# A four-layer decoder trunk on one core: where the residual shifts of the last layer stand on ScalarE, and where the forget decay stands on VectorE

## The chip, the cores and the metric

The kernel runs on one core of a Trainium2 chip. The metric is the device time of one execution in microseconds (us). TensorE (PE in the profile) does the matrix products, VectorE (DVE) and ScalarE (ACT) the work between them, GpSimd (POOL) a small part, and SyncE (SP) issues the transfers. Each engine runs its own list of instructions in order and waits on semaphores for the others.

## What is computed

272 tokens (16 meta tokens and 256 of the sequence) of width 1024 go through four layers. Each layer is a mixer and a gated feed-forward part, each with a residual and a layer norm. The mixers are of the kinds fox, swa, mla, fox: layer 0 and layer 3 are forgetting attention, the part that matters here.

```
def fox_mixer(h, w_in, b_f, w_o):
    proj = h @ w_in
    q, k, v, fg = jnp.split(proj, [hd, 2 * hd, 3 * hd], axis=-1)
    log_f = jax.nn.log_sigmoid((fg + b_f).astype(jnp.float32))
    c = jnp.cumsum(log_f, axis=1)
    o = dense_causal_attention(q, k, v, c)      # logits + c[t] - c[s]
    return o.reshape(B, L, hd) @ w_o
...
h = layer_norm(DEEPNORM_ALPHA * h + mix, ln1_g[i], ln1_b[i])
ffn = conv_glu_ffn(h, ...)
h = layer_norm(DEEPNORM_ALPHA * h + ffn, ln2_g[i], ln2_b[i])
```

The 16 forget gates of a token need `h @ w_in[:, 3072:]` in full precision, then a log-sigmoid and a running sum over the tokens. That sum is the decay.

## The kernel before

**Products and weights.** Tokens lie along the free dimension (272 columns), channels along the 128 partitions. Weights come from memory in units of 128 x 1024, through a ring of four buffers (`raw`, `w_hi`, `w_lo`). ScalarE rounds a unit to `w_hi` (L796, `split_hi`), VectorE subtracts to get `w_lo` (L1166 in `split_lo`), and TensorE makes each product of three passes, hi x hi, hi x lo and lo x hi (L376, L379, L380, `panel`; L415 to L429 in the leading panels that follow a layer norm chunk by chunk). One panel is 8 chunks x 3 passes = 24 matmuls into a PSUM bank. The splits run three units ahead of the panel (`AHEAD`). A split of a unit waits until TensorE has begun the panel that shows the ring buffer to be free (`w_used`). A new transfer waits for the `w_lo` of four units before.

**The fox stage.** Stage "v" makes 8 value panels (banks 0 to 3), stage "qk" 16 panels, queries and keys in turn (banks 0 and 1). VectorE copies each value panel out of its bank with `take_v` (L1356, "q_rope<-ps" in the rows, since the buffer is shared), which counts up `bank_free`. TensorE then turns the value to token order (L480, `value`), three panels late: value 0 after panel 3, value 4 after panel 7, and values 5, 6 and 7 within the first two panels of "qk". The first panel of "qk" waits for seven copies (`bank_free`, copy 6 among them, counted from 0).

**The gates.** After panel 2, TensorE computes the gate logits in full float32 (L608, 8 products that show as 16 rows). In layer 3 these read the residual `h` after its shift, so TensorE waits there for all eight `affine` instructions (L911), in which ScalarE adds the layer norm's beta to `h` for one chunk each. The panels themselves read `h_hi` and `h_lo`, which contain beta already. In layer 0 there is no such wait. Behind panel 3, ScalarE does five small instructions on 16 partitions (L933 to L937), and then VectorE does the rest of the log-sigmoid, the running sum (L1345) and two rounded copies of it in `dec` (L1348 and the subtraction behind it). The first scores of the stage (L502) read `dec`, after the first two panels of "qk".

**What sets the order.** The program of each engine is written out by hand. In the fox value stage, the loop of VectorE's `gemm` does for every panel j: the `split_lo` of a unit, then `before(i, j)`, then the wait for the panel, then the evicting copy. ScalarE's loop does for every panel m: `split_hi`, then three, three and two `affine` for m = 0, 1, 2 (layer 3 only), then the copies of turned values.

Of the kernel before, what the change touches and what calls it, by code (L numbers as in the profile page):

```python
# [31 lines left out]
DC = D // P  # L32
# [151 lines left out]
def build_program(nc, x, weights, consts, out):  # L184
    with ExitStack() as ctx:
        def sb(name, shape, dt=F32):
            return ctx.enter_context(nc.sbuf_tensor(name, shape, dt))
# [6 lines left out]
        h, squares = h_all[:, 0:DC], h_all[:, DC:DC + 2]  # L194
# [25 lines left out]
        y = sb("y", [P, 4, T])  # L220
        gated = sb("gated", [P, T])
# [73 lines left out]
        def bank(p, n=BANKS):  # L295
            return ps[:, p % n, 0:T]
# [17 lines left out]
        def turns(eng, n, emit, first=0):  # L314

            if n - first == 1:
                emit(first)
            elif n > first:
                with eng.Fori(first, n) as i:
                    emit(i)  # L320
# [466 lines left out]
        def _(act):  # L787
# [40 lines left out]
            def copy_value(m, where):  # L828
                act.wait_ge(v_turned, n_v[0] + m + 1)
                b = ps[:, where]  # L830
                act.activation(v_tok[0:16, 2, m * P:(m + 1) * P], b[0:16, 2 * P:3 * P], ACT.Copy)
                act.activation(v_tok[:, 0:2, m * P:(m + 1) * P],
                               b[:, 0:2 * P].rearrange("p (c n) -> p c n", c=2), ACT.Copy).then_inc(v_copied, 1)
# [33 lines left out]
            def split_panel(a, name, j):  # L867
                for u in units_of(a, name, 0, j):
                    split_hi(u)
# [37 lines left out]
            def affine(n, ks):  # L907

                for k in ks:
                    act.wait_ge(h_ready, 8 * (n + 1) + k + 1)  # L910
                    act.activation(h[:, k, :], h[:, k, :], ACT.Identity,  # L911
                                   bias=ln_par[:, n, 1, k:k + 1]).then_inc(affine_done, 1)
# [9 lines left out]
            for a, kind in enumerate(KINDS):  # L922
                if kind == "fox":
                    pq = LAYERS[a]["qk"][2]

                    def gate_act_ops():

                        z, mag, e, u1, lnu = (y[0:16, 0, :], y[0:16, 1, :], y[0:16, 2, :], y[0:16, 3, :],
                                              gated[0:16, :])
                        act.wait_ge(gate_done, n_fox + 1)  # L930
                        gb = CONST["gate_b"][0] + n_fox
                        bias = cst[0:16, gb:gb + 1]
                        act.activation(z, ps[0:16, 6, 0:T], ACT.Identity, bias=bias)  # L933
                        own.link(act.activation(mag, ps[0:16, 6, 0:T], ACT.Abs, bias=bias))
                        own.link(act.activation(e, mag, ACT.Exp, scale=-1.0))
                        own.link(act.activation(u1, e, ACT.Identity, bias=1.0))
                        act.activation(lnu, u1, ACT.Ln).then_inc(gate_act, 1)  # L937

                    for m in range(PAIRS):
                        split_panel(a, "v", m)  # L940
                        if a and m < 3:
                            affine(2 * a - 1, range(3 * m, min(DC, 3 * m + 3)))
                        if m == 1 and a == 0:
                            act.wait_ge(const_landed, 16)
                            act.wait_ge(init_done, INITS)
                        if m >= 3:
                            copy_value(m - 3, 4 + (m - 3) % 2)
                        if m == 3:
                            gate_act_ops()
# [211 lines left out]
        def _(dve):  # L1161
# [3 lines left out]
            def tt(out_, a_, b_, op):  # L1165
                return dve.tensor_tensor(out_, a_, b_, op)  # L1166

            def split_lo(u, slot):
                dve.wait_ge(hi_ready, u + 1)
                tt(w_lo[slot][:], raw[slot][:], w_hi[slot][:].bitcast(F32), ALU.subtract).then_inc(lo_ready, 1)  # L1170

            def split_units(layer, name, i, j):
                s, u0, _ = LAYERS[layer][name]
                for u in s.new_units(j):
                    first = u0 + u + AHEAD
                    if isinstance(i, int) and i * s.body_units + first >= N_UNITS:
                        continue
                    split_lo(i * s.body_units + first, first % RING)

            def gemm(layer, name, evac, links=0, before=None, straight=False, late=None):  # L1180

                s, u0, p0 = LAYERS[layer][name]

                def turn(i):
                    if links is not None:
                        own.turn(i, links)
                    for j in range(s.body):
                        ending = late is not None and i == s.turns - 1 and j == s.body - 1
                        last_unit = (s.units - 1 + u0 + AHEAD, (s.units - 1 + u0 + AHEAD) % RING)
                        if not ending:  # L1190
                            split_units(layer, name, i, j)
                        else:
                            for u in s.new_units(j)[:-1]:
                                if i * s.body_units + u0 + u + AHEAD < N_UNITS:
                                    split_lo(i * s.body_units + u0 + u + AHEAD, (u0 + u + AHEAD) % RING)
                            late()
                        if before is not None:
                            before(i, j)
                        dve.wait_ge(panel_done, i * s.body + (p0 + j + 1))
                        evac(i, j, bank(p0 + j + s.shift), i * s.body + (p0 + j))  # L1200
                        if ending and last_unit[0] < N_UNITS:
                            split_lo(*last_unit)

                if straight:
                    for i in range(s.turns):
                        turn(i)
                else:
                    turns(dve, s.turns, turn)
                if links is not None:
                    own.turned(s.turns)  # L1210
# [110 lines left out]
            for a, kind in enumerate(KINDS):  # L1321
                if kind == "fox":
                    pq = LAYERS[a]["qk"][2]

                    def decay():

                        z, mag, e, u1, lnu = (y[0:16, 0, :], y[0:16, 1, :], y[0:16, 2, :], y[0:16, 3, :],
                                              gated[0:16, :])
                        zero = squares[0:16, 0, :]
                        dve.wait_ge(gate_act, n_fox + 1)  # L1330
                        own.link(dve.tensor_scalar(u1, u1, -1.0, None, ALU.add))
                        own.link(dve.tensor_scalar(zero, u1, 0.0, None, ALU.is_equal))
                        tt(lnu, lnu, zero, ALU.add)
                        own.link(tt(u1, u1, zero, ALU.add))
                        own.link(dve.reciprocal(u1, u1))
                        own.link(tt(lnu, lnu, u1, ALU.mult))
                        own.link(tt(lnu, lnu, e, ALU.mult))
                        own.link(dve.tensor_scalar(z, z, -1.0, 0.0, ALU.mult, ALU.max))
                        own.link(tt(lnu, lnu, z, ALU.add))
                        own.link(dve.tensor_scalar(zero, zero, 0.0, 1.0, ALU.mult, ALU.add))  # L1340
                        if a == 0:
                            own.link(copy(pick[:], c("pick")))
                        row = scores[0:16, 0, :]
                        total = row[:, SCOL[2]:SCOL[3]]
                        own.link(dve.tensor_tensor_scan(total, zero, lnu, 0.0, ALU.mult, ALU.add))  # L1345
                        copy(row[:, SCOL[0]:SCOL[1]], total[:, 0:CHUNKS[0][1]])
                        own.link(copy(row[:, SCOL[1]:SCOL[2]], total[:, 0:CHUNKS[1][1]]))
                        own.link(copy(dec[0:16], row))  # L1348
                        tt(dec[32:48], row, dec[0:16].bitcast(F32), ALU.subtract).then_inc(decay_done, 1)
# [7 lines left out]

                    def before_v(i, j):

                        if i * 4 + j == 4:  # L1360
                            if a == 0:
                                dve.wait_ge(const_landed, 16)
                                dve.wait_ge(init_done, INITS)
                                own.link(dve.tensor_scalar(neg_sinks[:], c("sinks"), -1.0, None, ALU.mult))
                            decay()

                    gemm(a, "v", take_v, links=None, before=before_v, straight=True)
                    n_v += 8

                    def take_k(m):  # L1370
# [326 lines left out]
```

## Time and profile before

| | |
|---|---|
| median of 3 runs | 1399.6 us (1399.28 to 1401.74) |
| the profiled execution | 1400.15 us |
| its span, first to last instruction | 1398.3 us |
| mean granted TensorE clock | 0.984 of full speed |
| TensorE busy | 1333.4 us, 95% |
| VectorE, ScalarE, GpSimd busy | 945.4, 811.4, 231.7 us |

The profiled execution has 1.85 us outside its span. A busy TensorE is not one at its peak: matmuls are pipelined, and a row's duration overlaps the next row's. The pace is read from one start to the next. Starts are in us from the span's beginning.

### The profile page before, as it was taken

How to read it: one execution, taken by the hardware profiler on the slowest of the kernel's cores; microseconds unless marked ns; L12 is line 12 of the kernel's file. 1: busy time of each engine (PE TensorE's matmuls, PEld its weight loads, DVE VectorE, ACT ScalarE, POOL GpSimd, SP SyncE). 2: the span in 40 equal slices, each digit the busy share in tenths (PEclk: the TensorE clock that was granted, in tenths of full speed). 3: DMA queues.
4: the chain of work that ended last, by engine and by line, in shares of the span. 5: the costliest groups of instructions: out<-in, count | busy, mean ns of one | idle time of the engine just before them, and what ended most of it. 6: DMA issues, size and time to landing. Idle time of an engine off the chain costs nothing.

```text
span 1398.3 us, 30127 instructions
## 1 busy us (share of the span) xinstructions
PE 1333.4 (95%) x10433; PEld 1264.9 (90%) x10433; DVE 945.4 (68%) x1890; ACT 811.4 (58%) x1637; POOL 231.7 (17%) x216
## 2 busy tenths in 40 slices
PE   7899999999999999999977999999998999999997
PEld 6788999999977999999965899999997888999997
DVE  4665777765797777765684777776565566777754
ACT  5455676654666666654743567665454555766544
POOL 1000044420000044320010003433000000243400
PEclk9999999999999999999996999999999999999999
DMA  7332456556421456556431235655643333356662
GB/s 261 111 108 74 135 178 184 180 181 195 137 76 48 135 181 191 170 191 187 127 97 31 61 121 166 184 176 183 194 130 125 107 93 122 121 188 187 183 215 84
DMA packets 56867, 203.33 MB, mean 145 GB/s; under 512 B 6224, under 2 KB 8272, under 8 KB 56656
## 3 DMA queue, kind: packets, MB, share of 16 engines
q1 hardware_dynamic: 56784, 202.21, 46.2%
q8 instruction: 54, 0.88, 0.3%
q14 instruction: 29, 0.24, 0.0%
HBM read 201.13 MB, written 1.05 MB: 145 GB/s over the span
## 4 chain that ended last, share of the span: by engine, by line
PE 84%; DVE 7%; ACT 6%; issue 2%; DMA 1%; SPq 0%; DVEq 0%; ACTq 0%
PE ps L376 23%; PE ps L380 22%; PE ps L379 22%; PE ps L525 3%; PE ps L543 2%; DVE w_lo L1166 2%; PE ps L508 1%; PE ps L490 1%; ACT w_hi L796 1%; PE ps L415 1%; PE ps L421 1%; PE ps L418 1%; ACT probs L846 1%; DMA cst<-in_consts 1%; ACT L898 1%
## 5 line engine op out<-in xcount | busy, mean ns | idle before, releaser
L1166 DVE TENSOR_TENSOR w_lo<-raw,w_hi 128x1024 fp32r<-128x1024 f32 x378 | 462.5, 1225 | 251.6 <-ACT w_hi L796 250.0
L376 PE MATMUL ps<-h_hi,w_hi 128*128 128x272 f32 (+1 forms) x1752 | 511.2, 292 | 7.5 <-DVE q_rope L1356 4.9
L796 ACT ACTIVATE w_hi<-raw 128x1024 fp32r<-128x1024 f32 x378 | 396.8, 1051 | 188.9 <-PE ps L376 177.7
L380 PE MATMUL ps<-h_hi,w_lo 128*128 128x272 f32 (+1 forms) x1752 | 504.6, 288 | 0.0
L379 PE MATMUL ps<-h_lo,w_hi 128*128 128x272 f32 (+1 forms) x1752 | 503.2, 287 | 0.0
L376 PEld LDWEIGHTS ps<-h_hi,w_hi 128*128 128x128 f32 x1752 | 330.4, 189 | 15.5 <-issue 5.9
L379 PEld LDWEIGHTS ps<-h_lo,w_hi 128*128 128x128 f32 x1752 | 331.0, 189 | 0.3
L380 PEld LDWEIGHTS ps<-h_hi,w_lo 128*128 128x128 f32 x1752 | 330.5, 189 | 0.0
L376 PE MATMUL ps<-hid_hi,w_hi 128*128 128x272 f32 (+2 forms) x676 | 197.0, 291 | 2.7 <-DVE keys L1166 1.3
L380 PE MATMUL ps<-hid_hi,w_lo 128*128 128x272 f32 (+2 forms) x676 | 194.6, 288 | 0.0
L379 PE MATMUL ps<-hid_lo,w_hi 128*128 128x272 f32 (+2 forms) x676 | 194.6, 288 | 0.0
L1140 POOL TENSOR_TENSOR gated<-y 128x272 f32<-128x272 f32 x88 | 134.8, 1532 | 276.4 <-DVE y L1555 261.8
L1117 POOL TENSOR_TENSOR h<-h,y 128x272 f32<-128x272 f32 x24 | 17.9, 773 | 779.6 <-ACT y L895 779.6
L1090 ACT ACTIVATE y<-ps,cst 128x272 f32<-128x272 f32 x176 | 100.1, 569 | 65.6 <-PE ps L380 60.9
L376 PEld LDWEIGHTS ps<-hid_hi,w_hi 128*128 128x128 f32 x676 | 128.4, 190 | 4.8 <-DVE keys L1166 2.0
L379 PEld LDWEIGHTS ps<-hid_lo,w_hi 128*128 128x128 f32 x676 | 128.8, 191 | 0.1
L380 PEld LDWEIGHTS ps<-hid_hi,w_lo 128*128 128x128 f32 x676 | 128.7, 190 | 0.0
L846 ACT ACTIVATE probs<-scores,stats 16x16 f32<-16x16 f32 (+2 forms) x192 | 76.9, 401 | 58.9 <-DVE stats L1226 58.9
L1553 DVE SCALAR_TENSOR_TENSOR y<-ps,cst,y 128x271 f32<-128x271 f32 x176 | 87.4, 496 | 31.6 <-ACT y L1090 25.3
L1555 DVE SCALAR_TENSOR_TENSOR y<-ps,cst,y 128x270 f32<-128x270 f32 x176 | 87.8, 499 | 26.8 <-DVE y L1553 25.1
L380 PE MATMUL ps<-hid,w_lo 128*128 128x272 f32 (+1 forms) x288 | 82.2, 285 | 0.0
L379 PE MATMUL ps<-hid,w_hi 128*128 128x272 f32 (+1 forms) x288 | 82.1, 285 | 0.0
(159 smaller groups left out, 1722.9 us busy)
## 6 DMA issues: line engine op xcount, KB each, us to landing
raw<-in_weights SPq DMA_DIRECT2D x378, 512.0 KB, 3.6
cst<-in_consts SPq DMA_DIRECT2D x1, 1795.5 KB, 11.7
h<-in_x SPq DMA_DIRECT2D x2, 544.0 KB, 5.4
out<-h SPq DMA_DIRECT2D x8, 128.0 KB, 1.8
```

The lines of the kernel that those rows point to most:

```text
L376: m = pe.matmul(b, whi, xhi, start=n == 0, stop=False)
L379: pe.matmul(b, whi, xlo, start=False, stop=False)
L380: m = pe.matmul(b, wlo, xhi, start=False, stop=n == len(tiles) - 1)
L525: return pe.transpose(b[0:keys_n, col:col + q], pr[0:q, c0:c0 + keys_n], ident[0:q, 0:q])
L543: ins = pe.matmul(ps[HD * s:HD * s + HD, 6, lo:T], v_tok[:, t, col:col + HD], probs_t[:, s, c0:c0 + T - lo], start=n == 0, stop=n == 2)
L796: act.activation(w_hi[slot][:], raw[slot][:], ACT.Copy).then_inc(hi_ready, 1)
L846: ins = act.activation(probs[0:r, hn % 4, PCOL[ch]:PCOL[ch] + hi], scores[0:r, s, SCOL[ch]:SCOL[ch + 1]], ACT.Exp, scale=-1.0, bias=stats[ ...
L1090: act.activation(y[:, j, :], bank(pu + j), ACT.Identity, scale=col(2), bias=col(3)).then_inc(conv_begun, 1)
L1140: pool.tensor_tensor(gated[:], y[:, 2 * slot, :], y[:, 2 * slot + 1, :], ALU.mult).then_inc(gate_mul, 1)
L1166: return dve.tensor_tensor(out_, a_, b_, op)
L1553: own.link(dve.scalar_tensor_tensor(yj[:, 1:T], b[:, 0:T - 1], col(1), yj[:, 1:T], ALU.mult, ALU.add))
L1555: dve.scalar_tensor_tensor(yj[:, 2:T], b[:, 0:T - 2], col(0), yj[:, 2:T], ALU.mult, ALU.add).then_inc(bank_free, 1)
```

## The change

Two edits, both of order. The number of instructions on every engine is the same, and TensorE's order is the same.

1. ScalarE, layer 3: all eight `affine` stand behind the first `split_hi` of the value stage. Before, they were spread in groups behind its first, second and third.
2. VectorE, layers 0 and 3: `decay`, one block ahead of the eviction of panel 4, becomes four pieces. `decay_guard` stays there, `decay_quotient` (the reciprocal) stands ahead of the eviction of panel 5, `decay_steps` ahead of that of panel 6, and `decay_rows` (running sum and `dec`) behind the eviction of panel 7, ahead of the "qk" loop.

```
@@ -938,8 +938,8 @@
                     for m in range(PAIRS):
                         split_panel(a, "v", m)
-                        if a and m < 3:
-                            affine(2 * a - 1, range(3 * m, min(DC, 3 * m + 3)))
+                        if a and m == 0:
+                            affine(2 * a - 1, range(DC))
@@ -1322,22 +1322,32 @@
-                    def decay():
+                    def decay_guard():
+
                         dve.wait_ge(gate_act, n_fox + 1)
                         own.link(dve.tensor_scalar(u1, u1, -1.0, None, ALU.add))
                         own.link(dve.tensor_scalar(zero, u1, 0.0, None, ALU.is_equal))
                         tt(lnu, lnu, zero, ALU.add)
                         own.link(tt(u1, u1, zero, ALU.add))
+
+                    def decay_quotient():
+
                         own.link(dve.reciprocal(u1, u1))
+
+                    def decay_steps():
+
                         own.link(tt(lnu, lnu, u1, ALU.mult))
                         own.link(tt(lnu, lnu, e, ALU.mult))
                         own.link(dve.tensor_scalar(z, z, -1.0, 0.0, ALU.mult, ALU.max))
                         own.link(tt(lnu, lnu, z, ALU.add))
                         own.link(dve.tensor_scalar(zero, zero, 0.0, 1.0, ALU.mult, ALU.add))
+
+                    def decay_rows():
+
                         if a == 0:
                             own.link(copy(pick[:], c("pick")))
                         row = scores[0:16, 0, :]
@@ -1357,14 +1367,20 @@
                     def before_v(i, j):
-                        if i * 4 + j == 4:
+                        m = i * 4 + j
+                        if m == 4:
...
-                            decay()
+                            decay_guard()
+                        if m == 5:
+                            decay_quotient()
+                        if m == 6:
+                            decay_steps()
                     gemm(a, "v", take_v, links=None, before=before_v, straight=True)
+                    decay_rows()
                     n_v += 8
```

On ScalarE, this is the start of layer 3's value stage, behind the roundings of `h` (`h_hi`), as a difference from before to changed. `w_hi` rows are weight splits, `h<-h,cst` rows the residual shifts.

```order
 L906 ACTIVATE h_hi<-h,cst 128x272 x8
 L796 ACTIVATE w_hi<-raw 128x1024
-L911 ACTIVATE h<-h,cst 128x272 x3
-L796 ACTIVATE w_hi<-raw 128x1024
-L911 ACTIVATE h<-h,cst 128x272 x3
-L796 ACTIVATE w_hi<-raw 128x1024
-L911 ACTIVATE h<-h,cst 128x272 x2
-L796 ACTIVATE w_hi<-raw 128x1024
+L911 ACTIVATE h<-h,cst 128x272 x8
+L796 ACTIVATE w_hi<-raw 128x1024 x3
```

The shifts of chunks 3 to 7 now stand ahead of two weight splits that they stood behind.

On VectorE in layer 0, before: from the reciprocal to the eviction of panel 4 (the last row). Layer 3 has the same rows without the `pick` row.

```order
L1335 RECIPROCAL y<-y 16x272
L1166 TENSOR_TENSOR gated<-gated,y 16x272 x2
L1338 TENSOR_SCALAR y<-y 16x272
L1166 TENSOR_TENSOR gated<-gated,y 16x272
L1340 TENSOR_SCALAR h<-h 16x272
L1342 CAST pick<-cst 128x16
L1345 SCALAR_TENSOR_TENSOR scores<-h,gated 16x272
L1346 COPY scores<-scores 16x16
L1347 COPY scores<-scores 16x144
L1348 CAST dec<-scores 16x432
L1166 TENSOR_TENSOR dec<-scores,dec 16x432
L1356 COPY q_rope<-ps 128x272
```

The same place in the changed kernel, from the end of `decay_guard` to the weight split behind the eviction of panel 6. The copies "q_rope<-ps" are, in turn, the evictions of panels 4, 5 and 6.

```order
L1166 TENSOR_TENSOR y<-y,h 16x272
L1366 COPY q_rope<-ps 128x272
L1166 TENSOR_TENSOR w_lo<-raw,w_hi 128x1024
L1339 RECIPROCAL y<-y 16x272
L1366 COPY q_rope<-ps 128x272
L1166 TENSOR_TENSOR w_lo<-raw,w_hi 128x1024
L1166 TENSOR_TENSOR gated<-gated,y 16x272 x2
L1345 TENSOR_SCALAR y<-y 16x272
L1166 TENSOR_TENSOR gated<-gated,y 16x272
L1347 TENSOR_SCALAR h<-h 16x272
L1366 COPY q_rope<-ps 128x272
L1166 TENSOR_TENSOR w_lo<-raw,w_hi 128x1024
```

And right behind that, from the eviction of panel 7 to the first key copy of the "qk" stage.

```order
L1366 COPY q_rope<-ps 128x272
L1352 CAST pick<-cst 128x16
L1355 SCALAR_TENSOR_TENSOR scores<-h,gated 16x272
L1356 COPY scores<-scores 16x16
L1357 COPY scores<-scores 16x144
L1358 CAST dec<-scores 16x432
L1166 TENSOR_TENSOR dec<-scores,dec 16x432
L1166 TENSOR_TENSOR w_lo<-raw,w_hi 128x1024 x2
L1390 COPY keys<-ps 128x272
```

The running sum and the two `dec` rows moved from ahead of the eviction of panel 4 to behind that of panel 7. The reciprocal and the five steps after it now stand behind one and two evictions.

## Rows read from the trace of the kernel before

**Rows 1.** The page, busy us (share of the span) and instructions.

```profile
PE 1333.4 (95%) x10433; PEld 1264.9 (90%) x10433; DVE 945.4 (68%) x1890; ACT 811.4 (58%) x1637; POOL 231.7 (17%) x216
```

**Rows 2.** Waits, PE: who waited for whom, us in total, times, longest.

```profile
PE ps L376 <- DVE q_rope L1356: 4.9, 2, 2.5
...
PE ps L608 <- ACT h L911: 3.6, 1, 3.6
...
PE ps L480 <- DVE q_rope L1356: 2.5, 2, 1.4
```

**Rows 3.** Timeline, PE, layer 0: start, us, line, operation, count, idle and releaser.

```profile
18.80 3.84 PE L608 MATMUL ps<-h,cst 128*16 128x272 f32 x16
22.57 0.39 PE L376 MATMUL ps<-h_hi,w_hi 128*128 128x272 f32 x1
...
38.96 0.29 PE L380 MATMUL ps<-h_hi,w_lo 128*128 128x272 f32 x1
40.69 0.49 PE L480 MATMUL ps<-cst,q_rope 128*16 128x128 f32 x3 [1.44 <-DVE q_rope L1356]
...
43.65 0.39 PE L376 MATMUL ps<-h_hi,w_hi 128*128 128x272 f32 x1 [2.47 <-DVE q_rope L1356]
...
52.82 0.63 PE L502 MATMUL ps<-dec,pick 128*128 128x432 f32 x2 [0.37 <-DVE keys L1374]
```

**Rows 4.** Timeline, DVE, layer 0, around the decay block.

```profile
32.48 0.29 DVE L1331 TENSOR_SCALAR y<-y 16x272 f32<-16x272 f32 x1
...
33.95 1.84 DVE L1335 RECIPROCAL y<-y 16x272 f32<-16x272 f32 x1
35.83 0.89 DVE L1166 TENSOR_TENSOR gated<-gated,y 16x272 f32<-16x272 f32 x2
...
37.86 0.17 DVE L1342 CAST pick<-cst 128x16 fp32r<-128x16 f32 x1
...
40.19 0.44 DVE L1356 COPY q_rope<-ps 128x272 f32<-128x272 f32 x1
...
43.16 0.44 DVE L1356 COPY q_rope<-ps 128x272 f32<-128x272 f32 x1
```

**Rows 5.** Timeline, DVE, layer 3: running sum and the eviction of panel 4.

```profile
1071.69 0.71 DVE L1345 TENSOR_TENSOR_SCAN scores<-h,gated 16x272 f32<-16x272 f32 x1
...
1073.81 0.44 DVE L1356 COPY q_rope<-ps 128x272 f32<-128x272 f32 x1
```

**Rows 6.** Timeline, PE, layer 3, at the gates and at the first qk panel.

```profile
1047.45 0.29 PE L429 MATMUL ps<-h_hi,w_lo 128*128 128x272 f32 x1
1051.32 2.00 PE L608 MATMUL ps<-h,cst 128*16 128x272 f32 x4 [3.59 <-ACT h L911]
...
1056.60 0.39 PE L376 MATMUL ps<-h_hi,w_hi 128*128 128x272 f32 x1
...
1077.27 0.39 PE L376 MATMUL ps<-h_hi,w_hi 128*128 128x272 f32 x1 [2.47 <-DVE q_rope L1356]
```

**Rows 7.** Timeline, ACT, layer 3: shifts and weight splits.

```profile
1044.86 1.33 ACT L911 ACTIVATE h<-h,cst 128x272 f32<-128x272 f32 x3
1047.20 1.06 ACT L796 ACTIVATE w_hi<-raw 128x1024 fp32r<-128x1024 f32 x1 [1.01 <-PE ps L425]
...
1050.35 0.92 ACT L911 ACTIVATE h<-h,cst 128x272 f32<-128x272 f32 x2
```

**Rows 8.** Windows: stretch, its us, then busy us of PE, PEld, DVE, ACT, POOL, granted clock, DMA share, GB/s.

```profile
44.00:48.00 4.00, 4.00 (x22) 4.00 (x21) 2.30 (x3) 1.06 (x1) 0.00 (x0) 0.57 0.88 294
1051.00:1054.00 3.00, 2.68 (x6) 0.88 (x7) 1.05 (x2) 0.27 (x1) 0.00 (x0) 0.50 0.69 232
1078.00:1082.00 4.00, 4.00 (x22) 3.98 (x21) 1.92 (x3) 0.82 (x1) 0.00 (x0) 0.57 0.84 286
709.70:716.00 6.30, 3.95 (x24) 3.07 (x23) 6.06 (x13) 0.82 (x1) 2.38 (x3) 1.00 0.00 0
```

**Rows 9.** Timeline, PE, latent attention of layer 2, inside the last of those windows.

```profile
713.86 0.70 PE L704 MATMUL ps<-y,cst 128*128 128x272 f32 x2 [2.22 <-DVE queries L1166]
```

More of the change, by code:

```diff
@@ L1323, in _ @@
                     pq = LAYERS[a]["qk"][2]
-                    def decay():
-                        z, mag, e, u1, lnu = (y[0:16, 0, :], y[0:16, 1, :], y[0:16, 2, :], y[0:16, 3, :],
-                                              gated[0:16, :])
-                        zero = squares[0:16, 0, :]
+                    z, mag, e, u1, lnu = (y[0:16, 0, :], y[0:16, 1, :], y[0:16, 2, :], y[0:16, 3, :],
+                                          gated[0:16, :])
+                    zero = squares[0:16, 0, :]
+                    def decay_guard():
                         dve.wait_ge(gate_act, n_fox + 1)
```

## The prediction

> **What bounds the kernel now.** I read the page first: TensorE is busy 95% of the span [rows 1], so a microsecond counts only where TensorE stands still or runs slowly. The list of TensorE's waits comes second. Three of its lines lie in the code that the change touches [rows 2]: the first "qk" panel waits twice for a value eviction, 2.5 us each time; the turn of value 4 waits for one (two waits, 1.4 us the longer); and the gate logits of layer 3 wait 3.6 us for the residual shifts. Third, the timelines of TensorE, VectorE and ScalarE around these waits show what is late. In layer 0 TensorE's last value panel ends at 38.96 + 0.29 = 39.25. It idles 1.44 us, turns value 4, idles 2.47 us, and starts the first "qk" panel at 43.65 [rows 3]. VectorE meanwhile goes through the decay block from 32.48 to 40.19, 7.7 us on 16 partitions, and only then starts the evictions [rows 4]. Panels 4, 5 and 6 had been finished long before. Layer 3 shows the same 2.47 us [rows 6].
>
> The fourth view is the windows, for the granted clock. It is at its upper level (2.4 GHz) in most of the program, and falls to the lower one (1.2 GHz) right after each of the three stalls: 0.57 as a mean over 44 to 48 and over 1078 to 1082, and 0.50 over 1051 to 1054 [rows 8]. So each stall is paid twice, as idle time and as slow matmuls behind it. The price of the second part can be read from the gates, which are the same work in both layers: they take 22.57 - 18.80 = 3.77 us in layer 0 at the full clock [rows 3] and 1056.60 - 1051.32 = 5.28 us in layer 3 at the lower one [rows 6], 1.51 us more. For the "qk" panels, a mean clock of 0.57 over 4.00 us is at most 4.00 x 0.43 = 1.7 us lost. I take 1.5 us for each of the three places.
>
> **Edit 1, the shifts in layer 3.** Three shifts take 1.33 us and the last row has its full 0.5 us, so one follows another every (1.33 - 0.50) / 2 = 0.415 us [rows 7]. Eight in a row from 1044.86 end at 1044.86 + 7 x 0.415 + 0.5 = 1048.27. Before, the last ended at 1050.35 + 0.92 = 1051.27 and TensorE started at 1051.32. The gates start 3.0 us earlier. TensorE's leading panels end at 1047.45 + 0.29 = 1047.74 [rows 6], so 0.6 us of idle stays out of 3.59, and the clock should not fall there: another 1.5 us. The cost is on ScalarE: the second weight split, which started at 1047.20 after 1.01 us of idle for TensorE, now starts at 1048.2, and the third stands directly behind it, ahead of no shift any more. The `w_lo` of the second moves by 1 us on VectorE, and so do the evictions of panels 1 and 2 queued behind them and the transfers that SP's queue issues on them. TensorE covers this with 3.77 us of gates and a value panel of about 3 us before it wants the second of those units, so I cost it at nothing. Without this cover it would be the 1 us. Edit 1 is worth 3.0 + 1.5 = 4.5 us.
>
> **Edit 2, the decay pieces.** The first "qk" panel waits for the eviction of panel 6, so I count what stands ahead of that copy on VectorE. The guard ends at 33.95. The reciprocal takes 35.83 - 33.95 = 1.88, the steps 37.86 - 35.83 = 2.03, the rows 40.19 - 37.86 = 2.33 (with the `pick` copy), and a pair of eviction and weight split (43.16 - 40.19) / 2 = 1.49 [rows 4]. Before: 33.95 + 1.88 + 2.03 + 2.33 + 2 x 1.49 = 43.17. After: the same sum without the rows, 33.95 + 1.49 + 1.88 + 1.49 + 2.03 = 40.84. TensorE follows 0.49 later (43.16 to 43.65), at 41.3. The gain in layer 0 is 2.33 us. In layer 3 the rows have no `pick` and take 1073.81 - 1071.69 = 2.12 us [rows 5]. That is the gain there.
>
> Where the stall goes: value 4 no longer waits, since the eviction of panel 4 starts at 33.95. Its turn follows the last value panel at once and ends near 39.6. What is late next is still the eviction of panel 6, so TensorE idles about 41.3 - 39.6 = 1.7 us once, against 1.44 + 2.47 = 3.91 us in two parts. Whether the clock still falls has to be bounded from both sides. It fell after 1.44 and 2.47 us of idle with only turns between them [rows 3, 8]. It stayed at 1.00 from 709.7 to 716.0 with an idle of 2.22 us inside [rows 8, 9]. The 1.7 us that stays is below that, so I take no fall: 1.5 us more in each layer. The other end is nothing.
>
> The Trainium skill ("TensorE: Matmul & The Clock Gate", section "Why this matters for your kernels") advises against idle gaps over about 3 us. The trace departs from it: no single gap at the "qk" panel was over 2.47 us, and the clock fell. By the page alone edit 2 could bring no clock back, since there was no long gap, and the sum would be 3 us smaller.
>
> The rows piece is the one with a new place: behind it on VectorE are now two weight splits and the first key copy, and TensorE's first scores wait for `dec`. In layer 0 the eviction of panel 6 starts at 40.84, that of panel 7 at 42.33. Its copy takes some 0.36, and the rows end at 42.69 + 2.33 = 45.0. The scores started at 52.82 [rows 3]; moved forward by 2.3 + 1.5 us they start at 49.0. So `dec` has 4.0 us of slack, the two splits and a key copy (about 2.8 us) fit behind it, and the cost is nothing. Without that cover each microsecond late is one in each layer.
>
> **The sum.** Edit 1 brings 3.0 + 1.5. Edit 2 brings 2.33 + 1.5 in layer 0 and 2.12 + 1.5 in layer 3. Together this is 11.95 us. From the profiled execution's 1400.15 us that gives 1388.2 us. That execution is 0.55 us above the median, so by the median it would be 1387.65. I put the time at 1388.0.
>
> **Rivals.**
> - *The clock still falls at the "qk" panel.* Between the last value panel's matmuls and the first of "qk" there remain a turn of 0.49 us and 1.7 us of idle, 2.2 us without an ordinary matmul, about as much as the 2.22 us that did no harm at 713.86. If the moment decides, one or both places lose their 1.5 us: 1389.5 or 1391.0. The Trainium skill (same page, "Part 4: PE-mode transpose") says that transposes do not count as busy in the usual way; that speaks for this rival. Chance 0.27.
> - *Gains given back downstream.* The latent stage of layer 2 has stretches at the lower clock too, and everything behind layer 0 starts 3.8 us earlier. Runs of before spread over 1399.28 to 1401.74, so such things move the time by 1 to 2.5 us: up to 1390.5, or down to 1385.5. Chance 0.10, either side.
> - *The idle belongs to something else.* If the gate's wait ended with something other than the shifts, or the "qk" panel's with its weights, edit 1 or 2 would bring nothing: 1388.0 + 4.5 = 1392.5 without edit 1 and 1388.0 + 7.45 = 1395.5 without edit 2. Against it: ScalarE ends the last shift at 1051.27, 0.05 us before TensorE starts, and the weights of the first "qk" panel were split a whole pair before its eviction. Chance 0.05.
> - *Slower: `dec` comes too late.* The rows piece stands behind all evictions, so if it ran so much longer there that it ended after 49.0, the scores of both layers would wait. It decides from 4.0 us of delay per layer. To end above 1399.6 it would have to eat 11.95 us on top, thus be (11.95 + 2 x 4.0) / 2 = 10 us late in each layer, five times its own length. At 12 us late each it would give 1388.2 + 2 x 8 = 1404. Chance 0.01.
>
> **How the numbers follow.** My forecast, 1388.0 with a range of its own of 1386.5 to 1389.5, gets 0.57. With the clock rival the time reaches 1391. Adding the spread on the low side and the far end of the downstream rival gives 1385.5 to 1391.8, with somewhat over 1 in 10 outside. A difference under 0.2%, 2.8 us, cannot be told from none. All cases but the last, and a combination of lost edits inside the fourth, are beyond that: faster 0.96, same 0.03, slower 0.01.
>
> **What would show it.** In the changed profile the wait of the gates for the shifts is under 1 us, the gates take 3.8 us, and the clock is at 1.00 behind them. Value 4 has no wait. The first "qk" panel of both layers waits once, 1.7 us, for a value eviction; the copy of panel 6 starts 2.3 us (layer 0) earlier. `dec` is ready at about 45 and the first scores of layer 0 start at 49.0. The prediction is wrong if the clock falls in these places, if the first scores wait for `dec`, or if TensorE waits for a weight split in layer 3's first four panels.

## The result: 1.0% faster, a little more than forecast, and the profile after

The changed kernel takes 1385.83 us in the median of four runs (1384.12 to 1387.86), the one before 1400.38 us (1399.28 to 1401.74, with a fourth run that was taken beside it): a ratio of 0.9896, 95% interval 0.9879 to 0.9914. The forecast was 1388.0, with 1386.5 to 1389.5 as the range of its own mechanism and 1385.5 to 1391.8 with the rivals added: the time lies outside the first and 0.3 us inside the second. The profiled execution took 1384.12 us, with a span of 1382.2 us, 16.1 us less than the one of before.

The page of the changed kernel: TensorE has 9.5 us less of busy time for the same 10433 instructions, so the single instruction took less on average.

```profile
PE 1323.9 (96%) x10433; PEld 1258.4 (91%) x10433; DVE 945.0 (68%) x1890; ACT 810.9 (59%) x1637; POOL 231.7 (17%) x216
```

TensorE's waits in the changed kernel (us in total, times, longest) answer to [rows 2]. The wait for the first "qk" panel is 1.8 and 1.5 us instead of 2.5 twice, that for the shifts 0.6 instead of 3.6, and the wait of value 4 is gone.

```profile
PE ps L376 <- DVE q_rope L1366: 3.3, 2, 1.8
...
PE ps L608 <- ACT h L911: 0.6, 1, 0.6
```

Its timeline of TensorE (start, duration, then the idle time ahead), layer 0 first and then layer 3 (from 1031.05 on), answers to [rows 3] and [rows 6].

```profile
39.14 0.49 PE L480 MATMUL ps<-cst,q_rope 128*16 128x128 f32 x3
41.38 0.40 PE L376 MATMUL ps<-h_hi,w_hi 128*128 128x272 f32 x1 [1.75 <-DVE q_rope L1366]
...
50.55 0.63 PE L502 MATMUL ps<-dec,pick 128*128 128x432 f32 x2 [0.36 <-DVE keys L1390]
...
1031.05 0.39 PE L415 MATMUL ps<-h_hi,w_hi 128*128 128x272 f32 x1 [0.57 <-ACT h_hi L906]
...
1040.93 3.84 PE L608 MATMUL ps<-h,cst 128*16 128x272 f32 x16 [0.58 <-ACT h L911]
1044.70 0.39 PE L376 MATMUL ps<-h_hi,w_hi 128*128 128x272 f32 x1
...
1063.26 0.40 PE L376 MATMUL ps<-h_hi,w_hi 128*128 128x272 f32 x1 [1.54 <-DVE q_rope L1366]
...
1070.92 0.63 PE L502 MATMUL ps<-dec,pick 128*128 128x432 f32 x2 [0.37 <-DVE keys L1390]
```

Layer 0 has its first "qk" panel at 41.38 (forecast 41.3). Its first scores (L502) start at 50.55 instead of 52.82: 2.27 us, the decay's part alone. In layer 3 the gates take 3.77 us (1040.93 to 1044.70) against 5.28, and from their end to the first "qk" panel it is 18.56 us against 20.67.

The windows of the changed kernel (columns as in [rows 8]; the mean granted clock, as a share of the upper level, is the third number from the end) show why: the clock fell again in layer 0, and did not in layer 3, neither at the gates nor at the first "qk" panel.

```profile
42.00:46.00 4.00, 4.00 (x22) 3.97 (x21) 3.83 (x9) 0.93 (x1) 0.00 (x0) 0.57 0.45 136
1041.00:1045.00 4.00, 4.00 (x18) 1.70 (x19) 3.06 (x4) 1.77 (x2) 0.00 (x0) 1.00 0.37 107
1060.00:1067.00 7.00, 5.46 (x45) 5.15 (x44) 6.70 (x15) 2.00 (x5) 0.00 (x0) 1.00 0.50 153
```

VectorE in layer 0 of the changed kernel, evictions of panels 4 to 7 (L1366), reciprocal (L1339), the start of the steps (the 0.89 row) and the weight split behind the rows piece, stands as it was counted from [rows 4], within 0.05 us.

```profile
34.00 0.44 DVE L1366 COPY q_rope<-ps 128x272 f32<-128x272 f32 x1
...
35.49 1.83 DVE L1339 RECIPROCAL y<-y 16x272 f32<-16x272 f32 x1
37.36 0.44 DVE L1366 COPY q_rope<-ps 128x272 f32<-128x272 f32 x1
...
38.85 0.89 DVE L1166 TENSOR_TENSOR gated<-gated,y 16x272 f32<-16x272 f32 x2
...
40.88 0.44 DVE L1366 COPY q_rope<-ps 128x272 f32<-128x272 f32 x1
...
42.37 0.43 DVE L1366 COPY q_rope<-ps 128x272 f32<-128x272 f32 x1
...
45.04 1.23 DVE L1166 TENSOR_TENSOR w_lo<-raw,w_hi 128x1024 fp32r<-128x1024 f32 x1
```

ScalarE runs the eight shifts in one piece of 3.40 us, as counted from [rows 7].

```profile
1037.48 3.40 ACT L911 ACTIVATE h<-h,cst 128x272 f32<-128x272 f32 x8
1040.79 1.99 ACT L796 ACTIVATE w_hi<-raw 128x1024 fp32r<-128x1024 f32 x2
```

**Where the 16.1 us went.** The span can be cut into stretches from one marker on TensorE to the next: from the start to the first scores of layer 0; from there to the first leading panel of layer 3 (L415 at 1038.42 before), called the middle stretch from here on; from there to the first scores of layer 3 (layer 3's stretch); and the rest. Two of the markers in the kernel before:

```profile
1038.42 0.39 PE L415 MATMUL ps<-h_hi,w_hi 128*128 128x272 f32 x1 [0.57 <-ACT h_hi L906]
...
1086.44 0.63 PE L502 MATMUL ps<-dec,pick 128*128 128x432 f32 x2 [0.36 <-DVE keys L1374]
```

| stretch | before | changed | difference |
|---|---|---|---|
| to the first scores of layer 0 | 52.82 | 50.55 | -2.27 |
| middle stretch, from there to layer 3's leading panels | 985.60 | 980.50 | -5.10 |
| from there to the first scores of layer 3 | 48.02 | 39.87 | -8.15 |
| from there to the end of the span | 311.86 | 311.28 | -0.58 |

Layer 3 gave 8.15 us against a forecast of 4.5 + 2.12 + 1.5 = 8.12. Layer 0 gave 2.27 of 3.83. The 5.10 us in between were not forecast, and no instruction differs there. 4.00 of them lie between two turns of the latent attention of layer 2, which each follow a wait of 5.7 us. The two rows of before, and then the two of the changed kernel:

```profile
738.12 0.80 PE L480 MATMUL ps<-cst,q_rope 128*16 128x128 f32 x3 [5.67 <-issue]
...
757.78 0.80 PE L480 MATMUL ps<-cst,q_rope 128*16 128x128 f32 x3 [5.68 <-issue]
```

```profile
735.58 0.80 PE L480 MATMUL ps<-cst,q_rope 128*16 128x128 f32 x3 [5.69 <-issue]
...
751.24 0.80 PE L480 MATMUL ps<-cst,q_rope 128*16 128x128 f32 x3 [5.69 <-issue]
```

From one turn to the other it is 19.66 us at a mean granted clock of 0.59 before, and 15.66 us at 0.83 in the changed kernel.

### The profile page after: what moved, and what is told of

It is laid out like the page before. It is cut to its first block, busy times and chain, and to the rows that moved or that the text cites. A ratio compares the mean times of both kernels' runs of the same rounds, so it can differ in the third digit from the quotient of the medians.

```text
span 1382.2 us, 30127 instructions
## 1 busy us (share of the span) xinstructions
PE 1323.9 (96%) x10433; PEld 1258.4 (91%) x10433; DVE 945.0 (68%) x1890; ACT 810.9 (59%) x1637; POOL 231.7 (17%) x216
## 4 chain that ended last, share of the span: by engine, by line
PE 80%; DVE 8%; ACT 6%; issue 3%; POOL 1%; DMA 1%; ACTq 0%; SPq 0%; DVEq 0%; POOLq 0%
PE ps L376 22%; PE ps L380 21%; PE ps L379 21%; PE ps L525 3%; PE ps L543 2%; DVE w_lo L1166 2%; PE ps L508 1%; ACT w_hi L796 1%; ACT probs L846 1%; PE ps L490 1%; PE ps L415 1%; POOL gated L1140 1%; PE ps L421 1%; PE ps L418 1%; DMA cst<-in_consts 1%
```

## The experiments

Medians are given with the range of the runs. Each group of runs has runs of the kernel before beside it, and the ratio is to these.

### Edit 1 alone

```
 (before)
-if a and m < 3:
-    affine(2 * a - 1, range(3 * m, min(DC, 3 * m + 3)))
+if a and m == 0:
+    affine(2 * a - 1, range(DC))
```

> The kernel before with edit 1 alone (the eight shifts of layer 3 behind the first weight split). My theory: the gates start 3.0 us earlier and run at the full clock (3.8 us against 5.3), so 4.5 us less than before, near 1395.9 us against a median of before of 1400.4; the decay stalls stay, with their fall of the clock. Rival A (the affine wait is worth only its idle time, the clock falls anyway): 3.0 us less. Rival B (the surplus that the changed kernel showed in the latent stage of layer 2 belongs to its position or its order): since nothing differs up to layer 3, the latent stage must then look exactly like that of before, six windows at the lower clock; if the surplus is chance from one execution to the next, the windows at the lower clock differ although the program up to there is the same.

Measured: 1392.46 us (1392.13 to 1396.66), before 1399.96, ratio 0.9955 (0.9939 to 0.9972), which is 3.9 to 8.5 us less; this contains the 4.5, though the medians lie 7.5 us apart. In the trace the gates start 9.89 us behind the first leading panel instead of 12.90 and take 3.77 us instead of 5.28: 4.5 us. The decay stall of layer 3 is as it was, but the clock falls sooner and for longer than in the trace of before: over the 7 us from 1.75 us ahead of the first "qk" panel it has a mean of 0.52, where before has 0.76. This takes back 0.89 us (10.06 us from that panel to the first scores, against 9.17), so layer 3's stretch is 44.38 us, only 3.64 less than before.

```profile
1068.00:1075.00 7.00, 5.25 (x23) 5.25 (x24) 4.41 (x6) 1.06 (x1) 0.00 (x0) 0.52 0.75 239
```

For rival B: up to layer 3 this is the kernel before, and yet the middle stretch takes 982.50 us, not 985.60. It varies without any change, and its 3.10 us are part of what the medians show beyond 4.5.

### Edit 2 alone

```
 (changed)
-if a and m == 0:
-    affine(2 * a - 1, range(DC))
+if a and m < 3:
+    affine(2 * a - 1, range(3 * m, min(DC, 3 * m + 3)))
```

> The kernel before with edit 2 alone (decay in four pieces in layers 0 and 3). My theory: 2.3 us in layer 0 and 2.1 us in layer 3 for certain, and 1.5 us more in each layer in which the clock does not fall at the first qk panel: between 4.4 and 7.4 us less than before, middle 5.9, near 1394.5. In the gates of layer 3 the wait of 3.6 us and the slow 5.3 us stay. Rival (the gains of the two edits are not additive, because the shorter layer 0 changes where the clock falls later): the sum of this gain and that of edit 1 alone differs from 14.5 us by more than 3 us.

Measured: 1392.19 us (1388.75 to 1394.39), ratio 0.9940 (0.9923 to 0.9957), 6.0 to 10.8 us less. The expected 4.4 to 7.4 us overlap this, though the medians lie 7.8 us apart. The two ratios multiply to 0.9955 x 0.9940 = 0.9895, and the changed kernel has 0.9896: nothing speaks against the edits adding, within intervals that are each 4.6 to 4.8 us wide. The trace: first scores of layer 0 at 50.36, with a fall of the clock as in the changed kernel; layer 3's stretch 44.58 us, 3.44 less than before (2.1 and the clock); 986.19 us between.

### Decay in two pieces

```
 (changed)
 if m == 4:
     ...
     decay_guard()
-if m == 5:
     decay_quotient()
-if m == 6:
     decay_steps()
```

> The changed kernel, but with the decay in two pieces only: guard, quotient and steps all ahead of the eviction of panel 4 as before, the rows behind that of panel 7. My theory: what counts is only how much stands ahead of the eviction of panel 6, which is the same as with four pieces, so the first qk panel starts at the same 41.4 us and the time is that of the changed kernel within 0.5 us (near 1386). Rival (the interleaving itself matters, since values 4 and 5 come free earlier and the stall lies in one part): the eviction of panel 4 starts at 37.9 instead of 34.0, value 4 still does not wait (it is wanted at 39.1), so at most a few tenths; if it is over 1 us slower, interleaving has a worth of its own.

Measured: 1388.57 us (1383.44 to 1390.07), ratio 0.9913 (0.9892 to 0.9933). The median lies 2.7 us above the changed kernel's, which by itself would meet the rival's mark of 1 us, but the intervals overlap and the trace puts the difference elsewhere. Timeline of TensorE, layer 0: the first "qk" panel waits 1.76 us and starts at 41.47, against 1.75 and 41.38.

```profile
39.22 0.49 PE L480 MATMUL ps<-cst,q_rope 128*16 128x128 f32 x3
41.47 0.40 PE L376 MATMUL ps<-h_hi,w_hi 128*128 128x272 f32 x1 [1.76 <-DVE q_rope L1366]
...
49.13 0.63 PE L502 MATMUL ps<-dec,pick 128*128 128x432 f32 x2 [0.37 <-DVE keys L1388]
```

Value 4 is turned without a wait here too. Layer 3's stretch is 39.87 us, the same as in the changed kernel. So in the fox layers two pieces are as good as four: only what stands ahead of the eviction of panel 6 counts. The clock did not fall in layer 0 this time, and the scores start 1.42 us before the changed kernel's, although the same instructions stand ahead of the eviction of panel 6. The middle stretch was slow, 986.10 us. That this has nothing to do with the pieces is not shown by one trace.

### Steps behind the evictions too

```
 (changed)
-if m == 6:
-    decay_steps()
 ...
 gemm(a, "v", take_v, ...)
+decay_steps()
 decay_rows()
```

> The changed kernel with the five steps moved too, behind the eviction of panel 7 ahead of the rows. My theory: the eviction of panel 6 starts at 38.9 instead of 40.9 us, before TensorE wants it, so the stall of 1.75 us at the first qk panel is gone and with it every fall of the clock there. On VectorE the rows still end near 45.1, so the two weight splits and the first key copy end near 47.8, later than TensorE wants the first scores (46.6): a new wait of about 1.2 us in place of 0.4. Net about 1.2 us less per layer, and 1.5 us more in a layer in which the clock fell: 2.4 to 5.4 us less than the changed kernel, near 1382. Rival (the stall only moves): the first scores wait the full 1.75 us more and the time is that of the changed kernel, 1386.

Measured: 1386.52 us (1381.88 to 1388.12), ratio 0.9898 (0.9879 to 0.9917). The expected 2.4 to 5.4 us under the changed kernel did not come: against 1385.83 the medians show no gain. The trace shows the mechanism as expected: no wait at the first "qk" panel in either layer, no fall of the clock, and the first scores waiting 1.24 us for the key copy, at 48.10.

```profile
48.10 0.62 PE L502 MATMUL ps<-dec,pick 128*128 128x432 f32 x2 [1.24 <-DVE keys L1389]
```

This is 2.4 us ahead of the changed kernel in layer 0 (0.9 us ahead of its repetition below, in which the clock did not fall), and layer 3's stretch is 38.52 us against 39.87, 1.35 less. The middle stretch took 986.79, 6.3 us more than in the trace of the changed kernel, which is more than the fox layers gained.

### The changed kernel again

> The changed kernel once more, unaltered, as a control beside the next three. Theory 1 (the surplus over the forecast of 12 us was chance: the latent stage of layer 2 had 17 us at the lower clock in that execution, 27 in the one of before): the median comes out near 1387.5, 12 to 13 us under before, and from the first scores of layer 0 to the first leading panel of layer 3 it takes anything from 980 to 987 us. Theory 2 (the surplus belongs to the change): again 14.5 us or more under before, and that stretch stays near 980.5.

Measured: 1383.88 us (1383.22 to 1385.27), before 1399.5, ratio 0.9889 (0.9871 to 0.9907). The median, 15.6 us under before, speaks for theory 2. The trace speaks for a mixture: the middle stretch took 982.41 us, again on the short side of the 980 to 987, and the clock did not fall in layer 0 (first scores at 48.98, where 49.0 had been forecast, and 1.57 us before the first trace of the same kernel). Over the two groups and the two-piece kernel, with the same timing in the fox layers, the medians are 1383.9, 1385.8 and 1388.6, which is 15.6, 14.6 and 11.4 us under the runs of before beside them. I take it that the change is worth 11 to 16 us, and these runs do not narrow it. The times of the 35 runs of before beside the experiments go with their mean granted clock, 0.982 to 0.990 (correlation -0.73), which fits a spread that comes from the clock.

### The latent stage filled

```
 (changed)
+def keep_warm(count, where):
+    for _ in range(count):
+        pe.matmul(ps[:, where, T:512], h_hi[:, 0, 0:P], h_hi[:, 1, 0:512 - T], ...)
 ...
 latent_panel(0, 0)
+keep_warm(16, 4)
 swap(gated[:], pa + 6)
 ...
 if m == 0:
+    keep_warm(12, 4)
     swap_rope(1)
 ...
+if m in (ROPE_AFTER, ROPE_AFTER + 1):
+    pe.wait_ge(o_split, PAIRS * a + m - ROPE_AFTER)
+    keep_warm(36, 6)
```

> The changed kernel, with extra matmuls on TensorE (into unused columns, their results are not read) inside its four long waits in the latent stage of layer 2: 16, 12, 36 and 36 of 240 columns. No work is left out and the waits themselves stay. Theory 1 (the clock of that stage explains both the surplus and the spread of the runs): the granted clock stays at its upper level there, the stretch from the first scores of layer 0 to layer 3 falls under 980 us, to about 973, and the spread of the runs shrinks to 2 or 3 us; time near 1377. Theory 2 (the stage is held by VectorE and the clock there costs nothing): the clock stays up, the stretch does not change, the time is that of the changed kernel. Third possibility: the extra matmuls do not fit in the waits and push the stage back, slower by up to 5 us.

Measured: 1381.50 us (1379.22 to 1384.12), ratio 0.9876 (0.9856 to 0.9897). The median is 2.4 us under the changed kernel's beside it, with intervals that overlap. The added wait (`o_split`) keeps the filler out of a PSUM bank that VectorE still reads. The windows of the stage, 695 to 775 us, one line each, of the kernel before, the changed kernel and this one, show the mean granted clock in the third number from the end.

Kernel before:

```profile
695.00:775.00 80.00, 61.09 (x362) 48.84 (x361) 56.26 (x168) 33.33 (x97) 4.40 (x4) 0.83 0.25 73
```

Changed kernel:

```profile
695.00:775.00 80.00, 60.56 (x398) 48.49 (x396) 60.88 (x192) 35.22 (x109) 4.40 (x4) 0.89 0.24 73
```

Latent stage filled:

```profile
695.00:775.00 80.00, 70.70 (x530) 59.38 (x528) 63.73 (x202) 38.78 (x124) 4.40 (x4) 1.00 0.23 71
```

The clock stays at its upper level throughout, and the middle stretch takes 977.13 us. In every trace this stage is the only part of the middle stretch with a lower clock: cut into 50 us from the first scores of layer 0 on, all the other slices are at 1.00. In the table over all traces the stretch gets shorter as the clock rises, in the main though not row by row, while TensorE's instructions in it are the same in all but the filled ones:

| trace | clock, 695 to 775 | middle stretch, us |
|---|---|---|
| edit 2 alone | 0.81 | 986.19 |
| before | 0.83 | 985.60 |
| two pieces | 0.83 | 986.10 |
| steps behind | 0.83 | 986.79 |
| edit 1 alone | 0.87 | 982.50 |
| key copy first (below) | 0.87 | 981.10 |
| stalls filled (below) | 0.89 | 982.42 |
| changed, repeated | 0.89 | 982.41 |
| changed | 0.89 | 980.50 |
| shifts first (below), filled | 0.98 | 978.09 |
| both (below), filled | 1.00 | 977.73 |
| latent stage filled | 1.00 | 977.13 |

So theory 1 holds for the mechanism: the surplus of the changed kernel's trace over the forecast is granted clock in the latent stage. Its size was less than I gave it: 977, not 973. The ends of the waits stay where VectorE's rotary work puts them (its last row ahead of the first turn ends at 734.21, the turn starts at 734.31). What is left idle is 0.9 us at the swaps and 1.7 us at the turns, where it had been 2.2 to 2.7 and 5.7. TensorE's timeline of this run has the turns.

```profile
734.31 0.49 PE L480 MATMUL ps<-cst,q_rope 128*16 128x128 f32 x3 [1.67 <-issue]
748.49 0.49 PE L480 MATMUL ps<-cst,q_rope 128*16 128x128 f32 x3 [1.68 <-issue]
```

The spread of the runs did not shrink in this kernel (4.9 us, where 2 to 3 were expected).

### Key copy first

```
 (steps behind)
 split_units(a, "qk", 0, 2 * m)
+if m == 0:
+    take_k(m)
 split_units(a, "qk", 0, 2 * m + 1)
-take_k(m)
+if m:
+    take_k(m)
```

> The kernel of the run with the steps behind, in which the first scores waited 1.24 us for the first key copy, with one more change: in the first round of the qk loop the key copy stands ahead of the second weight split on VectorE. My theory: the key copy is then only held by its panel, the wait falls from 1.24 to about 0.4 us, 0.8 us less in each layer, 1.7 us in all against that run (1386.5), near 1384.8. Rival (the split that now stands behind is late for its own panel): TensorE waits for w_lo two panels later and nothing is gained.

Measured: 1380.94 us (1379.42 to 1385.25), ratio 0.9872 (0.9851 to 0.9893). First scores at 47.14 with a wait of 0.37 us, 0.96 us ahead of the run before; layer 3's stretch 38.06 us instead of 38.52. Together this is 1.4 us, 1.7 expected. The medians lie 5.6 us apart, and the traces show where the larger part may come from: 981.10 against 986.79 us in the middle stretch. No later wait for a weight split appeared.

```profile
47.14 0.62 PE L502 MATMUL ps<-dec,pick 128*128 128x432 f32 x2 [0.37 <-DVE keys L1389]
```

### Both

> The run with the key copy first and the filled latent stage in one kernel: the gains add, since they lie in different layers. With theory 1 on the latent stage near 1374, with theory 2 near 1384.

Measured: 1376.68 us (1376.38 to 1377.14), ratio 0.9838 (0.9820 to 0.9855): 1.6% under before. Its edits are those of the last two sections. The middle stretch takes 977.73 us and layer 3's 38.07. With no stall left at the first "qk" panels and the latent stage filled, the five runs lie within 0.8 us, where the eleven of before, in the same group, lie within 6.5 (1395.86 to 1402.36). This is the shrinking that theory 1 asked for. It is not secured: five runs of a kernel with both places filled or closed as well (the last experiment) lie within 3.1 us, four of them within 0.8.

### The stalls filled in the order of before

```
 (before)
+if m == 7:
+    keep_warm(10)
 if m >= 3:
     value(m - 3)
+if m == 7:
+    keep_warm(18)
 if m == 2:
     if a:
+        keep_warm(28)
         pe.wait_ge(affine_done, 8 * 2 * a)
```

> The kernel before, in its own order, with extra matmuls on TensorE (240 columns, unused results) inside the three stalls: 28 ahead of the gates of layer 3, 10 and 18 around the turn of value 4 in both fox layers. No wait is taken away. It measures the clock's part of the forecast by itself. My theory: the stalls keep their ends (first qk panel at 43.7 us in layer 0, gates 12.9 us behind the first leading panel in layer 3), but the granted clock stays up behind them, the gates take 3.8 instead of 5.3 us, the first scores come 1.5 us earlier in each fox layer; 4.5 us less in all, near 1395.2, while the latent stage keeps its own spread. Rival (the fall does not cost what I took, or comes whatever TensorE does in the stall): less than 1.5 us in all.

Measured: 1391.75 us (1390.67 to 1395.11), before 1397.99, ratio 0.9952 (0.9938 to 0.9967), 4.6 to 8.7 us less. The fox layers account for a little under the lower end; in the trace the middle stretch, which has no filler, is shorter too, 982.42 against 985.60 us. The first "qk" panel starts at 43.76, as before (43.65), but the first scores at 51.41 instead of 52.82, 1.41 us earlier. In layer 3 the gates start 12.90 us behind the leading panel, as before, and take 3.84 us in their row; its stretch is 44.99 us instead of 48.02, 3.03 less. Together this is 4.44 us, against 3 x 1.5 in the forecast. The windows are at full clock, in the layer 0 place and at the gates (and at the "qk" panel of layer 3, 1070 to 1080).

```profile
44.00:48.00 4.00, 4.00 (x34) 3.96 (x34) 2.41 (x3) 1.99 (x6) 0.00 (x0) 1.00 0.90 267
1048.00:1054.00 6.00, 6.00 (x40) 4.35 (x38) 1.40 (x2) 1.06 (x1) 0.00 (x0) 1.00 0.25 88
```

This run shows the clock's part of the forecast by itself: nothing was moved, and only what TensorE did in the stalls differs. The rival, under 1.5 us in all, is out.

### Shifts ahead of the first split

```
 (both)
 for m in range(PAIRS):
+    if a and m == 0:
+        affine(2 * a - 1, range(DC))
     split_panel(a, "v", m)
-    if a and m == 0:
-        affine(2 * a - 1, range(DC))
```

> The fastest kernel so far (steps behind, key copy first, latent stage filled) with the eight shifts of layer 3 ahead of the first weight split instead of behind it. My theory: they end 0.9 us earlier, before TensorE has done its leading panels, so the wait of 0.6 us at the gates goes; the split ends 3.4 us later, but TensorE wants that unit only behind the 3.8 us of gates: 0.5 us less, near 1376.1, which only the trace of layer 3 can show. Rival (that split was the tighter one): TensorE waits for w_lo of its fourth panel, and it is the same or slower by up to 1 us.

Measured: 1376.09 us (1375.65 to 1378.78), ratio 0.9847 (0.9826 to 0.9867); the medians cannot tell it from the last. The trace can: the gates start without a wait, 9.25 us behind the leading panel instead of 9.88, and layer 3's stretch is 37.41 us instead of 38.07. No wait for a split took its place.

```profile
1034.31 3.84 PE L608 MATMUL ps<-h,cst 128*16 128x272 f32 x16
```

## Why the prediction was right, and where its parts were off

**Edit 1 (3.0 + 1.5 us): right in both terms.** The shifts took 3.40 us in one piece (3.41 counted), TensorE waited 0.58 us (0.6), and the gates took 3.77 us. Edit 1 alone showed the same. The split that moves behind the shifts cost nothing: no trace with this edit has a wait for a weight split in layer 3's value stage. Even the first split could move (the last experiment), so the cover that I named is real and larger than it was needed.

**Edit 2, order (2.33 and 2.12 us): right.** Measured 2.27 in layer 0 and 20.67 - 18.56 = 2.11 in layer 3. The reason holds, and the two-piece run sharpens it: the gain is the length of what no longer stands ahead of the eviction of panel 6, which is the rows piece (2.33 counted). The finer cutting of the rest adds nothing that a trace shows.

**Edit 2, clock (1.5 us in each layer): right in layer 3, not in the profiled layer 0.** The prediction named a fall of the clock as a sign of being wrong, and for layer 0 of the profiled execution it was: 9.17 us from the first "qk" panel to the first scores, as before, where 7.66 is what the full clock takes. The size is right (stalls filled: 1.41 us in layer 0), but that the clock stays up after 1.7 us of idle was decided on one row [rows 9], and a single case does not settle it. In the five traces that keep this stall (changed twice, edit 2 alone, two pieces, latent stage filled) it fell in 2 of 10 places, both in layer 0. With the old stall in two parts (3.9 us in layer 0, 3.5 in layer 3) it fell in 4 of 4 (before, edit 1 alone), and without a stall or with a filled one in 0 of 10. So the first rival (0.27) is real for a part of the executions. It was rightly a chance per place, not a verdict for both. The section of the Trainium skill that I weighed ("TensorE: Matmul & The Clock Gate", "Why this matters for your kernels") is again departed from: the clock fell behind a single gap of 1.75 us.

**`dec` not late: right.** The rows piece ended at 45.04 (45.0 forecast), and the first scores waited 0.36 us for the key copy, as before. The slower rival has nothing for it. The cover showed its limit one step on: with the steps behind as well, the first scores waited 1.24 us for the key copy. (A delay of 10 us, which that rival needed, is four times the length of the rows piece, not five; its chance does not hang on this.)

**The downstream rival was given too little.** I had put it at 0.10 and at up to 2.5 us. The middle stretch varies by 6 us between traces of the same instructions, with the granted clock of the latent stage. Of the 16.1 us between the two profiled executions, 10.4 lie in the fox layers (2.27 + 8.15), 5.10 in that stretch, and 0.58 at the end, where all traces lie between 311.2 and 311.9 us and which I did not follow. The step that failed is the term that I left out of the sum: TensorE's four long waits in the latent stage stood in the same list of waits, and what the clock does behind them should have been priced with them. In the medians the error is small (forecast 11.6 under the median of 1399.6, measured 14.5 under 1400.38). That the time is inside the stated range is in part luck: the fox layers of the profiled execution gave 1.5 us less than the 11.95 of the sum, the rest of the program 5.7 us more, and only the allowance for the spread brought the range down to 1385.5. Whether an earlier start of the stage makes a higher clock in it more likely stays open: the changed kernel had 0.89 in both of its traces, the two kernels with the same layer 0 order or timing (edit 2 alone, two pieces) had 0.81 and 0.83.

## What to carry to other kernels

When a consumer waits for one eviction, count only what stands ahead of that eviction in its engine's order, and move the longest block that nobody needs yet behind it; cutting the rest finer earned nothing here. Price each TensorE stall twice, as idle time and as the slow matmuls behind it, treat the second as a chance where the stall is short (2 of 10 places here), and look for such stalls in the whole program, since the clock behind them differs from run to run. Where a stall cannot be closed, filling it with matmuls that nobody reads gives back the second price: 4.4 us here, in the old order.

## What the runs showed of the hardware that was not expected

The clock's fall behind a stall is not a fixed price. Around the end of the old stall of layer 3 the granted clock averaged 0.76 over 7 us in one trace and 0.52 over the same 7 us in another, and the first cost 1.5 us and the second 2.4 (from the first "qk" panel to the first scores 9.17 and 10.06 us, against 7.66 at full clock). In the latent stage, where products alternate with waits of 2 to 6 us, it averaged anything from 0.81 to 0.89 over 80 us with the same instructions. Some 100 matmuls of 240 columns, placed in those waits, brought 1.00 (0.98 in one of three traces) and took 2 to 10 us off the stretch, although TensorE had more to do.
